# The last projection of the first FFN as seven block products in place of eight, in two sweeps over its weights

## The reference

```python
def conv_ffn(h, w_up, dw_w, w_down):
    u = causal_dwconv(h @ w_up, dw_w)
    a, v = jnp.split(u, 2, axis=-1)
    return (jax.nn.silu(a) * v) @ w_down
...
        y = conv_ffn(h, ffn_w_up[l], ffn_dw_w[l], ffn_w_down[l])
        x = x + g_c * rms_norm(y, cm_post_g[l])
```

## Time and profile before

| | before |
|---|---|
| median of 3 runs | 1629.94 us (1627.71 to 1634.13) |
| profiled execution, first to last instruction | 1628.6 us |
| TensorE busy | 1601.9 us, 98% of the span |
| VectorE busy | 931.5 us, 57% |
| ScalarE busy | 626.4 us, 38% |
| GpSimd busy | 188.0 us, 12% |
| mean granted TensorE clock | 0.992 |
| down1, from its first matmul to the first of the next stage | 121.6 us, GpSimd busy 1.3 us of it |

### The profile page before, as it was taken

The page is one execution under the profiler, slowest core; times in us unless marked ns, Lnnn a source line. Parts: engine busy times, 40 slices in busy tenths (PEclk is TensorE's granted clock), DMA queues, the critical chain, the costliest instruction groups (busy, mean ns, idle before and its releaser), DMA issues.

```text
span 1628.6 us, 20633 instructions
## 1 busy us (share of the span) xinstructions
PE 1601.9 (98%) x7892; PEld 1317.6 (81%) x7892; DVE 931.5 (57%) x1311; ACT 626.4 (38%) x826; POOL 188.0 (12%) x121
## 2 busy tenths in 40 slices
PE   6999999999999999999999999999999999999998
PEld 5888788788887888888888877778788888888887
DVE  5579554458897644445323777777355555556233
ACT  5433453242235533334223523353534433334223
POOL 1110033110002011011000001320123110111000
PEclk9999999999999999999999999999999999999999
DMA  9332123118653233332223243222123333333221
GB/s 330 92 113 94 53 77 104 53 52 285 207 182 106 57 95 103 103 88 92 104 103 103 60 125 91 83 78 78 53 78 103 93 101 103 99 83 103 104 103 52
DMA packets 189159, 170.46 MB, mean 105 GB/s; under 512 B 9544, under 2 KB 176805, under 8 KB 189093
## 3 DMA queue, kind: packets, MB, share of 16 engines
q1 hardware_dynamic: 171168, 150.16, 30.0%
q10 hardware_dynamic: 16948, 16.89, 3.2%
q0 software_dynamic: 976, 2.51, 0.5%
HBM read 165.54 MB, written 2.10 MB: 103 GB/s over the span
## 4 chain that ended last, share of the span: by engine, by line
PE 92%; DVE 3%; ACT 2%; DMA 2%; issue 1%; SPq 0%; ACTq 0%; DVEq 0%
PE bank L1378 21%; PE bank L1380 20%; PE bank L1379 20%; PE bank L1393 7%; PE bank L1395 7%; PE bank L1394 7%; PE bank L1480 1%; PE bank L2011 1%; PE bank L1723 1%; PE bank L1386 1%; DMA w_raw<-in_w_in 1%; DVE w_lo L2068 1%; PE bank L1388 1%; PE bank L1387 1%; PE bank L1996 1%; DMA work<-in_ada_w 1%
## 5 line engine op out<-in xcount | busy, mean ns | idle before, releaser
L1378 PE MATMUL bank<-h_hi,w_hi 128*128 128x512 f32 (+1 forms) x1424 | 556.8, 391 | 2.8 <-DVE w_lo L2068 2.0
L1380 PE MATMUL bank<-h_hi,w_lo 128*128 128x512 f32 (+1 forms) x1424 | 548.7, 385 | 0.0
L1379 PE MATMUL bank<-h_lo,w_hi 128*128 128x512 f32 (+1 forms) x1424 | 548.0, 385 | 0.0
L2068 DVE TENSOR_TENSOR w_lo<-w_raw,w_hi 128x2048 fp32r<-128x2048 f32 x112 | 256.6, 2291 | 263.7 <-ACT w_hi L762 263.0
L762 ACT ACTIVATE w_hi<-w_raw 128x2048 fp32r<-128x2048 f32 x129 | 246.3, 1909 | 262.2 <-PE bank L1395 180.3
L1378 PEld LDWEIGHTS bank<-h_hi,w_hi 128*128 128x128 f32 x1424 | 267.6, 188 | 72.2 <-issue 16.1
L1380 PEld LDWEIGHTS bank<-h_hi,w_lo 128*128 128x128 f32 x1424 | 267.8, 188 | 54.2
L1379 PEld LDWEIGHTS bank<-h_lo,w_hi 128*128 128x128 f32 x1424 | 268.0, 188 | 52.1 <-issue 1.0
L1393 PE MATMUL bank<-w_hi,y_hi 128*128 128x512 f32 x352 | 137.8, 391 | 0.0
L1395 PE MATMUL bank<-w_lo,y_hi 128*128 128x512 f32 x352 | 137.0, 389 | 0.0
L1394 PE MATMUL bank<-w_hi,y_lo 128*128 128x512 f32 x352 | 137.0, 389 | 0.0
(11 more groups left out here) (310 smaller groups left out, 1892.4 us busy)
## 6 DMA issues: line engine op xcount, KB each, us to landing
w_raw<-in_w_in SPq DMA_DIRECT2D x94, 512.0 KB, 4.5
w_raw<-in_ffn_w_up SPq DMA_DIRECT2D x44, 512.0 KB, 5.0
w_raw<-in_w_up SPq DMA_DIRECT2D x44, 512.0 KB, 4.6
work<-in_ada_w ACTq DMA_DIRECT2D x16, 1024.0 KB, 7.8
w_raw<-in_ffn_w_down SPq DMA_DIRECT2D x22, 512.0 KB, 4.0
w_raw<-in_w_down SPq DMA_DIRECT2D x22, 512.0 KB, 3.7
work<-in_ada_w SPq DMA_DIRECT2D x8, 1024.0 KB, 12.6
w_raw<-in_w_o SPq DMA_DIRECT2D x8, 512.0 KB, 4.4
```

The source lines that it names most:

```text
L1378: pe.matmul(dst, w_hi[s][:, at:at + n], hi, start=first, stop=False, skip_group_check=onto)
L1379: pe.matmul(dst, w_hi[s][:, at:at + n], lo, start=False, stop=False, skip_group_check=onto)
L1380: return pe.matmul(dst, w_lo[s][:, at:at + n], hi, start=False, stop=last, skip_group_check=onto)
L2068: dve.tensor_tensor(w_lo[u % 2][:, :], raw[u % 2][:, :], w_hi[u % 2][:, :].bitcast(FP32), ALU.subtract)\
```

## The change

The three matrices are cut in two by two blocks: the hidden activations by tokens (0 to 255, 256 to 511) and by the two hidden tiles of a unit, the weights by those tiles and by output halves. The product is formed with seven block products (Strassen's scheme in a form with few sums) instead of eight.

- There are two sweeps over the 11 pairs of hidden tiles, 22 units g in all. The first sweep makes four products for each token tile m of a half (24 matmuls a unit), the second makes three (18 a unit).
- The products need sums of blocks. For each unit of the first sweep, GpSimd makes three sums of 128x256 in the hidden pair (`hidden_sums`) and one of 128x512 in the weights (`weight_sum`), and VectorE one of 128x1024 (`weight_sums`). In the second sweep, GpSimd makes two of 128x256 and one of 128x1024, and VectorE one of 128x512. They are made before the split in high and low parts (`down_hi`, `down_low`, `hidden_hi`, `hidden_lo`).
- The weights are loaded twice: 768 KB a unit in the first sweep, 1 MB in the second, in four buffers. Two of them lie in `work`, over the buffers of the convolution, so units 2 and 3 are loaded once the last hidden tile is written.
- Between the sweeps ScalarE copies two banks of each m aside (`aside`), and VectorE puts four sums of 128x512 in place (`between`).
- Units 20 and 21 are interleaved so that banks come out one after the other; two banks (5 and 7) are complete after the first sweep.
- `rows_turned("down1", "res", 0)` comes behind the last matmul of the stage.
- The semaphores of both FFNs are shared, with other counts; the work of the second FFN is the same.

```diff
...
+        PAIR = FT // 2
+        BEFORE = {"1": 0, "2": 1}
+        DOWN = U["down1"]
...
+        raw_at = [raw[0], raw[1], area(FT * S + 4 * S, UNIT), area(FT * S, UNIT)]
...
+        QUAD = S // 2
+        FIRST = ((0, 0, 0), (3, 3, 5), (2, 1, 1), (1, 2, 4))
+        SECOND = ((1, 1, 0), (0, 2, 1), (2, 0, 4))
...
+            def down_rows(w_down):
+                for g in range(FT):
+                    u, dst, r = DOWN + g, raw_at[g % 4], g % PAIR * 2 * P
+                    if g < 2:
+                        before(u)
+                    elif g < 4:
+                        sp.wait_ge(sem("hid"), FT + 1)
+                    else:
+                        sp.wait_ge(parted[u % 2], u // 2 - 1)
+                    put(u, dst[:, 0:D], w_down[r:r + P, :])
+                    if g < PAIR:
+                        put(u, dst[:, D:D + S], w_down[r + P:r + 2 * P, S:2 * S])
+                    else:
+                        put(u, dst[:, D:2 * D], w_down[r + P:r + 2 * P, :])
+            down_rows(A["ffn_w_down"][0])
...
-                pool.nop().then_inc(sem("hid" + n), 1)
...
+                for j in range(2):
+                    hidden_sums(j)
+                tile(PAIR - 1, 0)
+                weight_sum(0)
+                weight_sum(1)
+                tile(PAIR - 1, 1)
+                for g in range(2, FT):
+                    hidden_sums(g)
+                    weight_sum(g)
+            def hidden_sums(g):
+                j, step = g % PAIR, sem("pool_step")
+                pair, e = pair_of(j), stage(j)
+                b11, b12, b21, b22 = (pair[:, q * QUAD:(q + 1) * QUAD] for q in range(4))
+                if g < PAIR:
+                    pool.wait_ge(sem("hid"), 2 * j + 3)
+                    if j >= 2:
+                        pool.wait_ge(sem("down_lo1"), j - 1)
+                    pool.tensor_tensor(e[:, 0:QUAD], b12, b22, ALU.subtract).then_inc(step, 1)
+                    pool.wait_ge(step, g + 1)
+                    pool.tensor_tensor(e[:, QUAD:2 * QUAD], b11, e[:, 0:QUAD], ALU.subtract)
+                    pool.tensor_tensor(b12, b11, b12, ALU.subtract).then_inc(sem("hid_sums"), 1)
+                else:
+                    pool.wait_ge(sem("down_lo1"), j + 1)
+                    pool.tensor_tensor(b12, b12, b22, ALU.add).then_inc(step, 1)
+                    pool.wait_ge(step, g + 1)
+                    pool.tensor_tensor(b12, b21, b12, ALU.subtract).then_inc(sem("hid_sums"), 1)
+            def weight_sum(g):
+                w = raw_at[g % 4]
+                pool.wait_ge(loaded[g % 4], loaded_at(DOWN + g))
+                if g < PAIR:
+                    ins = pool.tensor_tensor(w[:, 2 * S:3 * S], w[:, S:2 * S], w[:, 2 * S:3 * S], ALU.add)
+                else:
+                    ins = pool.tensor_tensor(w[:, 0:2 * S], w[:, 0:2 * S], w[:, 2 * S:4 * S], ALU.add)
+                ins.then_inc(sem("weight_sum"), 1)
...
@@ -1130,7 +1236,7 @@
...
+                def down_hi(g):
+                    act.wait_ge(sem("weight_sums"), g + 1)
+                    act.wait_ge(w_used, DOWN + (g - 2 if g == FT - 2 else g - 1))
+                    dst, src = down_weights(w_hi, h_hi, g), raw_at[g % 4]
+                    if g < PAIR:
+                        ins = act.activation(dst[:, :], src[:, :], ACT.Copy)
+                    else:
+                        ins = act.activation(dst[:, 0:3 * S], src[:, S:4 * S], ACT.Copy)
+                    ins.then_inc(hi_done, 1)
+                def hidden_hi(g):
+                    j = g % PAIR
+                    act.wait_ge(sem("hid_sums"), g + 1)
+                    if g >= 2:
+                        act.wait_ge(w_used, DOWN + (2 if g >= FT - 2 else max(g - 3, 0)))
+                    dst, pair = parts_at(y_hi, h_hi, g), pair_of(j)
+                    if g < PAIR:
+                        act.activation(dst[:, 0:S], pair[:, 0:S], ACT.Copy)
+                        ins = act.activation(dst[:, S:2 * S], stage(j), ACT.Copy)
+                    else:
+                        ins = act.activation(dst[:, 0:3 * QUAD], pair[:, QUAD:4 * QUAD], ACT.Copy)
+                    ins.then_inc(sem("down_hi1"), 1)
+                def aside(m):
+                    if m:
+                        act.wait_ge(w_used, DOWN + PAIR)
+                    else:
+                        act.wait_ge(sem("first_done"), 1)
+                    for c, dst in ((0, sq), (4, tbuf)):
+                        act.activation(dst[:, m, :], bank[T["down1"][c + 2 * m].bank][:, :], ACT.Copy).then_inc(sem("aside"), 1)
...
                 up_units(FT // 2 - 1, last=True)
+                if n == "1":
+                    down_hi(1)
+                    hidden_hi(2)
+                    hidden_hi(3)
+                    for g in range(1, FT - 1):
+                        if g == PAIR:
+                            aside(1)
+                        down_hi(g + 1)
+                        if g + 3 < FT:
+                            hidden_hi(g + 3)
+                        if g == PAIR - 1:
+                            aside(0)
+                    split(DOWN + FT)
+                    return
...
+                def product(g, m, kinds):
+                    whole = g < PAIR
+                    w_h, w_l = down_weights(w_hi, h_hi, g), down_weights(w_lo, h_lo, g)
+                    p_h, p_l = parts_at(y_hi, h_hi, g), parts_at(y_lo, h_lo, g)
+                    for part, weight, c in kinds:
+                        t = T["down1"][c + 2 * m]
+                        if g == 0:
+                            wait_free(pe, t)
+                        if g == PAIR:
+                            pe.wait_ge(*{0: (sem("aside"), 2 * m + 1), 1: (sem("mid"), 4 * m + 3), 4: (sem("mid"), 4 * m + 4)}[c])
+                        a, b = part * QUAD + m * P, weight * S
+                        hi, lo = p_h[:, a:a + P], p_l[:, a:a + P]
+                        pe.matmul(bank[t.bank][:, :], hi, w_h[:, b:b + S], start=g == 0, stop=False, skip_group_check=True)
+                        pe.matmul(bank[t.bank][:, :], lo, w_h[:, b:b + S], start=False, stop=False, skip_group_check=True)
+                        mm = pe.matmul(bank[t.bank][:, :], hi, w_l[:, b:b + S], start=False, stop=not whole, skip_group_check=True)
+                        if g == FT - 1:
+                            done(mm, t)
+                    return mm
+                def down_ready(g):
+                    weights_ready(DOWN + g)
+                    pe.wait_ge(sem("down_lo1"), g + 1)
+                if n == "1":
+                    for g in range(FT - 2):
+                        down_ready(g)
+                        mm = product(g, 0, FIRST if g < PAIR else SECOND)
+                        if g == PAIR - 1:
+                            mm.then_inc(sem("first_done"), 1)
+                        mm = product(g, 1, FIRST if g < PAIR else SECOND)
+                        mm.then_inc(w_used, 1)
+                    a, b = FT - 2, FT - 1
+                    c11, c21, c12 = SECOND
+                    down_ready(a)
+                    product(a, 0, (c11, c21))
+                    product(a, 1, (c11, c21))
+                    product(a, 0, (c12,))
+                    down_ready(b)
+                    product(b, 0, (c11, c21))
+                    product(b, 1, (c11, c21))
+                    product(b, 0, (c12,))
+                    product(a, 1, (c12,)).then_inc(w_used, 1)
+                    product(b, 1, (c12,))
+                    return
...
-            ffn("1", under_last)
+            ffn("1")
+            rows_turned("down1", "res", 0)
...
-                        if not begun:
+                        if last and k and n == "1":
+                            hidden_lo(1)
+                            down_low(0)
+                        elif not begun:
                             lo(up + k + 1, i * 2)
-                        if last:
+                            if last and n == "1":
+                                hidden_lo(0)
+                        if last and n == "2":
                             part_lo(k)
...
+                        if last and n == "1":
+                            weight_sums(k)
+                def weight_sums(g):
+                    w = raw_at[g % 4]
+                    dve.wait_ge(sem("weight_sum"), g + 1)
+                    if g < PAIR:
+                        ins = dve.tensor_tensor(w.rearrange("p (a b n) -> p a b n", a=2, b=2)[:, :, 1, :],
+                                                w[:, S:3 * S].rearrange("p (a n) -> p a n", a=2),
+                                                w[:, 0:S].unsqueeze(1).broadcast_to([P, 2, S]), ALU.add)
+                    else:
+                        ins = dve.tensor_tensor(w[:, S:2 * S], w[:, 0:S], w[:, S:2 * S], ALU.add)
+                    ins.then_inc(sem("weight_sums"), 1)
+                def down_low(g):
+                    u, src = DOWN + g, raw_at[g % 4]
```

(100 more changed lines are left out.)

42 lines of the change are left out of this document (21 added, 21 removed).

## The result

After the change the kernel takes 1678.69 us (median of 4 runs, 1677.29 to 1679.48), before 1629.68 (median of 4): ratio 1.0288, 95% interval 1.0261 to 1.0315. The forecast was 1673, its range 1655 to 1698. The profiled execution has a span of 1677.7 us, 49.1 more than before. Nearly all of that lies in the down1 stage: the next stage begins at 946.47 in place of 898.57, 47.9 us later; the up stage ends at about 777 in both. One execution of the kernel called the floor, at 4553 us, is a slow one and is left out of its ratio.

A forecast was written before the change was run, and what follows sets the result against it. TensorE bounds the kernel before; VectorE's and GpSimd's summed times were to bound the changed stage. Start and sweeps +39.0, end +3.6, on 1628.6 give 1671.2, plus 1.3 for the median: 1673 us, range 1655 to 1698.

The forecast's parts named there:

- Removed: In the down1 stage, 66 of TensorE's 528 matmuls fall away, worth 15.0 us.
- The lock: In down1's units, VectorE and GpSimd exclude each other: 7.29 and 6.45 us a unit against TensorE's 5.44 and 4.08.
- the 0.60 of the sum: In down1's units, the 0.60 us counted for each of GpSimd's 256-column sums.
- The start: In down1's first units, TensorE waits 1.2 us before unit 0 and 9.2 before unit 1; unit 2 starts at +27.0.
- VectorE's low part at 778.2: Before down1's first unit, VectorE's low part of the weights ends at 778.2, so TensorE waits 1.2 us.
- The end: Behind down1's last matmul, the next stage starts 5.5 us later in place of 1.9: +3.6 us.
- Sum: Over the kernel, 39.0 + 3.6 = +42.6 us, a span of 1671.2 us.
- The clock: Rival: TensorE's clock falls as well in down1's sweeps, 1694 or 1720 us; chance 0.12.
- The rival's price of 21 us: Cost of TensorE's clock falling through down1's second sweep: +21 us, 1694 us; chance of the clock falling too 0.12.
- The other signs: In down1: stage some 164 us, unit 1 14 to 16 us after unit 0, GpSimd's 512 columns well over 1.3.
- No exclusion: Rival: in down1, VectorE and GpSimd don't hold each other up: +7.7 us, 1638 us; chance 0.10.
- Faster: Rival: down1's start hides and the engines overlap, 10 us gained, 1620 us; chance 0.03.

The follow-up runs named there:

- the floor: Changed kernel with GpSimd's sums cut to 8 columns, VectorE's start reordered, unit 2 loaded early, the second bank sums moved ahead at the turn: 1628.91 us.
- the copies: Changed kernel with each of GpSimd's sums made a copy of one of its inputs to the same output: 1643.98 us, ratio 1.0088.
- the kernel with more products: Changed kernel with the second matmul of each product issued twice in units 3 to 18: 1679.08 us, ratio 1.031.
- the two kernels in which nothing is held: Changed kernel with GpSimd's sums cut to 8 columns, 1635.45 us, and with them made constant fills of the same outputs, 1637.65 us.

## Why the prediction was right, and by how much it missed

- **Removed: right.** TensorE has 66 matmuls less on the page (7826 against 7892).
- **The lock: right, and shown.** 7.29 and 6.45 us a unit were forecast and measured. That the figures agree to 0.01 is partly luck. I took 0.14 from every duration but GpSimd's for 256 columns, which I had between 0.59 and 0.70: less 0.14 that is 0.45 to 0.56, and the sums would have been 6.84 to 7.17 and 6.15 to 6.37. Unheld, it measured 0.74 here, so the 0.60 of the sum was right and its working was not. The nine units to the second sweep took 64.8 us by TensorE (809.33 to 874.08; 65.6 forecast), from there to the end of the products 65.0 (64.9 forecast). Taking GpSimd's work away, adding to it, making it write-only and moving it each moved the units' paces as the sum says, but for the copies' second sweep.
- **The start: mis-sized by some 4 us.** Unit 0 waited 4.2 us in place of 1.2, and unit 2 started 32.4 us behind 776.97 in place of 28.2. The step that was off is "VectorE's low part at 778.2": `hidden_lo(1)`, ahead of `down_low(0)` in VectorE's order, was left out of the chain, and the last hidden tile was taken to end as before (780.22 + 1.30). It ended at 786.03, since its convolution stands behind `down_low(0)`, and the loads with it.
- **The end: mis-sized by 1.9 us.** From the last product to the next stage 7.4 us (939.1 to 946.47), 5.5 forecast. The squares of bank 1 to the next stage took 8.65 us (8.72 forecast), but began at 937.82, 1.3 us before the products' end in place of 3.2. That is the whole 1.9. ScalarE still had the split of the next stage's weights before them, which waited for its load, and then a table load:
```profile
934.01 1.92 ACT L868 ACTIVATE w_hi<-w_raw 128x2048 fp32r<-128x2048 f32 x1 [1.68 <-DMA w_raw<-in_w_in]
935.94 1.28 ACT L872 ACT_TABLE_LOAD   x1
```
The 16 transposes ran at the lower clock, 3.35 us, but this cost nothing here: in the kernel with more products they took 2.41 us, and the next stage still began at 946.41.
- **Sum.** 3.4 of start and sweeps, 1.9 of the end and 1.2 behind the stage make the 6.5 us between the spans 1671.2 and 1677.7. These 1.2 lie in the last 77.7 us of the kernel (76.5 before), in a stage that the change leaves alone; the granted clock is 0.98 there in place of 0.99. Why was not looked into.
- **The clock: it fell, and that decided nothing.** I had written that the forecast is wrong if the clock of the stage is under 1. It was 0.88 and the forecast held: that test was too strict, as a unit waits for VectorE anyway, which the kernel with more products shows. The rival's price of 21 us rested on a fall through the whole second sweep; it was 0.87 from 885 to 925. For the same reason TensorE was busy for 78% of the stage, and not for the two thirds that I had named as a sign: at the lower clock a matmul takes 0.63 us for 0.39. The other signs came: 165.3 us for some 164, unit 1 15.6 us behind unit 0, and GpSimd's 512 columns at 1.63 us on average for 1.27 unheld.
- **The other rivals.** "No exclusion" was to give 1638; the two kernels in which nothing is held gave 1635.45 and 1637.65. "Faster" needed the start hidden too; in the floor kernel most of it is (4.4 us of waits are left), and the time was level, not 1620.

## What to carry to other kernels

Before giving VectorE and GpSimd work for the same stretch, add their times, each less the 0.14 us that lies beside the other, if VectorE's instructions have two operands in SBUF and GpSimd's read from it; compare the sum, not the larger, with what TensorE needs. If the sum is over, moving GpSimd's part to VectorE is worth trying first, since VectorE does it in less time (0.42 against 0.74 us for 256 columns, neither held). And a product saved on TensorE is worth its pitch only while the additions that pay for it fit beside the products left: here 24 or 18 matmuls a unit no longer cover them.

## What the runs showed of the hardware beyond what was expected

- A held instruction counts as busy for all its waiting: GpSimd's 1024 columns averaged 3.65 us for 2.35, and it shows 125 us in a stage where its instructions, none held, would take 9 x 3.49 + 11 x 3.83 + 1.3 = 75.
- GpSimd's fills (0.31, 0.53 and 0.96 us for 256, 512 and 1024 columns) hold nobody and are held by nobody, its copies (0.40, 0.61 and 1.04 us) do both.
- In this stage too a VectorE operation with one operand in a bank is not held. Between the sweeps one takes 0.70 us in the middle of GpSimd's sum of 1024 columns, while one with both operands in SBUF, begun at 880.00, ends 0.56 us behind the end of GpSimd's next sum (881.27):
```profile
872.49 3.77 POOL L818 TENSOR_TENSOR work<-work 128x1024 f32<-128x1024 f32 x1
...
874.66 0.70 DVE L2927 TENSOR_TENSOR bank<-bank,sq 128x512 f32<-128x512 f32 x1
...
880.00 1.83 DVE L2931 TENSOR_TENSOR bank<-tbuf,sq 128x512 f32<-128x512 f32 x1
```
- TensorE's clock is at 0.50 from 795 to 800, around the end of its pause of 7.4 us, and at 1.00 again from 800 to 805; in the kernel with more products, whose matmuls fill most of the short pauses, it is 1.00 in both middle windows.
